# Delta rule stage: inverses of both chunks of a tile in one load, scalings in one load per chunk, each over 128 partitions instead of 64

## The reference

```python
    kk = jnp.einsum('bhnid,bhnjd->bhnij', k, k)
    lower = jnp.where(strict, beta[..., :, None] * kk * decay, 0.0) + jnp.eye(blen, dtype=f32)
    ...
    def step(s, xs):
        u_c, w_c, qk_c, qd_c, kt_c, gt_c = xs
        v_new = u_c - jnp.einsum('bhld,bhde->bhle', w_c, s)
        o_c = jnp.einsum('bhld,bhde->bhle', qd_c, s) + jnp.einsum('bhij,bhje->bhie', qk_c, v_new)
        s = s * gt_c[..., None, None] + jnp.einsum('bhld,bhle->bhde', kt_c, v_new)
        return s, o_c
```

## Time and profile before

| | us |
|---|---|
| three runs | 3799.37, 3775.93, 3805.12 |
| median | 3799.37 |
| the profiled execution, its own time | 3786.45 |
| its span, first to last instruction | 3784.6 |
| mean granted clock of TensorE | 0.953 of full |
| delta stage, from GpSimd's first step in it to its first step in the next | 1770.78 to 2136.54 |

### The profile page before, as it was taken

The page is one execution under the profiler, slowest core; times in us unless marked ns, Lnnn a source line. Parts: engine busy times, 40 slices in busy tenths (PEclk is TensorE's granted clock), DMA queues, the critical chain, the costliest instruction groups (busy, mean ns, idle before and its releaser), DMA issues. The chain is left out here.

```text
span 3784.6 us, 68890 instructions
## 1 busy us (share of the span) xinstructions
PE 3476.5 (92%) x26734; PEld 2979.7 (79%) x26734; DVE 2118.8 (56%) x4012; ACT 1362.6 (36%) x2626; POOL 1028.3 (27%) x1315
## 2 busy tenths in 40 slices
PE   7999999969999999994788569999976999999999
PEld 7999999957877788883777557888865888888887
DVE  6777777638978776932334336666654323233232
ACT  5544554433223232111455406666643111111111
POOL 4222222148988444300577600000000000000000
PEclk9999999989999999996798869999988999999999
DMA  5333333345347444335988222222246111121210
GB/s 158 107 104 111 108 112 107 86 133 179 93 128 213 136 138 121 102 99 118 231 244 248 68 65 96 71 85 72 84 152 224 67 60 67 60 72 59 67 67 35
DMA packets 322211, 429.81 MB, mean 114 GB/s; under 512 B 188587, under 2 KB 206283, under 8 KB 317310
## 3 DMA queue, kind: packets, MB, share of 16 engines
q1 hardware_dynamic: 321926, 425.94, 38.0%
HBM read 268.23 MB, written 160.25 MB: 113 GB/s over the span
## 5 line engine op out<-in xcount | busy, mean ns | idle before, releaser
L88 PE MATMUL b_psP<-b_w_hi,b_xT_hi 128*128 128x512 f32 x1320 | 518.8, 393 | 47.1 <-DVE b_xT_lo L1188 30.1
L89 PE MATMUL b_psP<-b_w_lo,b_xT_hi 128*128 128x512 f32 x1320 | 516.6, 391 | 0.0
L90 PE MATMUL b_psP<-b_w_hi,b_xT_lo 128*128 128x512 f32 x1320 | 516.2, 391 | 0.0
L88 PE MATMUL a_psG<-a_xT_hi,a_w_hi 128*128 128x256 f32 (+1 forms) x1632 | 467.8, 287 | 10.3 <-DVE a_xT_lo L559 9.4
L90 PE MATMUL a_psG<-a_xT_hi,a_w_lo 128*128 128x256 f32 (+1 forms) x1632 | 459.6, 282 | 0.0
L89 PE MATMUL a_psG<-a_xT_lo,a_w_hi 128*128 128x256 f32 (+1 forms) x1632 | 459.5, 282 | 0.0
L88 PEld LDWEIGHTS b_psP<-b_w_hi,b_xT_hi 128*128 128x128 f32 x1320 | 249.6, 189 | 105.7 <-DVE b_xT_lo L1188 53.8
L88 PEld LDWEIGHTS a_psG<-a_xT_hi,a_w_hi 128*128 128x128 f32 x1632 | 309.3, 189 | 26.2 <-DVE a_xT_lo L559 9.8
L576 DVE SCALAR_TENSOR_TENSOR a_act<-a_raw,a_taps,a_act 128x256 f32<-128x256 f32 x576 | 308.6, 536 | 20.5
L90 PEld LDWEIGHTS a_psG<-a_xT_hi,a_w_lo 128*128 128x128 f32 x1632 | 309.6, 190 | 0.0
L89 PEld LDWEIGHTS a_psG<-a_xT_lo,a_w_hi 128*128 128x128 f32 x1632 | 309.5, 190 | 0.0
(11 more groups left out here) (376 smaller groups left out, 7398.5 us busy)
## 6 DMA issues: line engine op xcount, KB each, us to landing
rows_b<-b_rows SPq DMA_DIRECT2D x165, 256.0 KB, 2.2
b_x_full<-xT SPq DMA_DIRECT2D x78, 512.0 KB, 4.0
qkvB<-a_act SPq DMA_DIRECT2D x16, 1536.0 KB, 5.1
d_conv_T<-qkvB SPq DMA_DIRECT2D x16, 1536.0 KB, 11.5
xT<-a_x_full SPq DMA_DIRECT2D x33, 512.0 KB, 5.1
h_mixed<-mixed SPq DMA_DIRECT2D x33, 512.0 KB, 4.0
out<-h_y SPq DMA_DIRECT2D x33, 512.0 KB, 2.9
a_x<-in_x_prompt SPq DMA_DIRECT2D x32, 512.0 KB, 4.6
```

What stands on the lines that cost most here:

```text
L88: nc.tensor.matmul(out, x_hi, w_hi, start=first, stop=False)
L89: nc.tensor.matmul(out, x_hi, w_lo, start=False, stop=False)
L90: return nc.tensor.matmul(out, x_lo, w_hi, start=False, stop=last)
```

## The change

In `load`, the loads of a tile's scalings and matrices are written otherwise. Before, a loop over the two halves of the partitions issued for each half one load of scalings (both chunks, the half's heads, one source row repeated for 64 partitions) and one of matrices (one chunk, 64 partitions). Now a loop over the two chunks issues for each one load of scalings over all 128 partitions, and one load brings the matrices of both chunks to all 128 partitions. The bytes and where each of them ends up are the same. A tile's semaphore now counts three loads instead of four.

```diff
@@ -1418,7 +1418,7 @@
     W = H * C
     HW = W // 2
     BUFS, ZBUFS = 6, 8
-    LOADS = 4
+    LOADS = 3
     with ExitStack() as stack:
         ph = Phase(nc, stack)
 
@@ -1531,11 +1531,12 @@
                     sp.wait_ge(t_o, 2 * 2 * (t - BUFS + 1))
                     sp.wait_ge(g_qd, t - BUFS + 1)
                 ok = c_in[b]
-                for e in range(2):
-                    half = slice(e * C, (e + 1) * C)
-                    sp.dma_start(sc[b][half, :, :, :, :],
-                                 d.kqrow[2 * t:2 * t + 2, e * PAIRS:(e + 1) * PAIRS].partition_broadcast(C)).then_inc(ok, 16)
-                    sp.dma_start(UQ[b][half, :, :, :], d.UQ[:, 2 * t + e]).then_inc(ok, 16)
+                for c in range(2):
+                    sp.dma_start(sc[b][:, c, :, :, :].rearrange("p a x i -> p (a x i)"),
+                                 d.kqrow[2 * t + c].rearrange("(e a) x i -> e (a x i)", e=2).unsqueeze(1)
+                                 .to_broadcast([2, C, PAIRS * 2 * C])).then_inc(ok, 16)
+                sp.dma_start(UQ[b][:, :, :, :].rearrange("p h x i -> p (h x i)"),
+                             d.UQ[:, 2 * t:2 * t + 2].rearrange("j e h x i -> e j (h x i)")).then_inc(ok, 16)
                 if t >= ZBUFS:
                     sp.wait_ge(g_out, t - ZBUFS + 1)
                 sp.dma_start(za[z][:, :], d.rows_b[t * P:(t + 1) * P, 0:W]).then_inc(za_in[z], 16)
```

## The result

The changed kernel takes **4288.3 us** in the median of four runs (4285.44 to 4292.61); the kernel before took 3802.24 beside it. The ratio is **1.129**, with a 95% interval of 1.123 to 1.135: 13% slower. The forecast was 4263 us in a range of 4180 to 4600. The profiled execution is one of the four, 4285.44 us with a span of 4283.6.

A forecast was written before the change was run, and what follows sets the result against it. The changed delta stage was taken to be bound by loads on two DMA engines: 32 tiles at 24.6 us make 787 us, with the tail +473; 3786.45 + 473 + 4 for a slower clock = 4263 us, range 4180 to 4600.

The forecast's parts named there:

- The stage alone is touched: Nothing outside the delta stage moves, apart from 4 us for a slower clock in the next; the stage gets 473 us longer.
- Issues at nothing: SP in the delta stage issues three loads a tile instead of four; put at 0, at most 19 us.
- The cut by the smaller outermost count: New sc and UQ loads count 2 outermost in DRAM, 128 in SBUF; the smaller binds, so two DMA engines carry them.
- 24.6 us a tile: Delta stage: each of two engines carries 606,208 B a tile at 24.6 GB/s; 32 tiles make 787 us.
- the 15.4 of the mix: Lower bound in GB/s for an engine's rate, from the delta stage's busy mix of loads before; it would give 39.4 us a tile.
- The tail: After the last load lands, GpSimd, about five tiles behind, needs 36 us, plus 8 for slow clock and 4 to the next stage.
- What would show it: Signs in the delta stage: DMA 2 tenths near 95 GB/s, line 1611 every 24 to 25 us, long GpSimd waits, clock near 0.5.
- Rival A: Delta-stage loads still use sixteen engines, at 405 GB/s, so compute decides: -47 us, 3739 us; chance 0.10.

The follow-up runs named there:

- e1_matrices_only: Against the kernel before, only the matrices (UQ) come in one load over 128 partitions, scalings as before; 4040.95 us, ratio 1.062.
- e2_scalings_only: Against the kernel before, only the scalings (sc) come in two loads over 128 partitions, matrices as before; 4042.62 us, ratio 1.063.
- q4_other_rows: The changed kernel with 4 instead of 2 outermost on the DRAM side, reading other rows; 3982.23 us, ratio 1.047 to the kernel before.
- rows_together: The changed kernel with matrices and scalings each read from 128 rows lying together in DRAM, other rows; 3756.44 us, ratio 0.987 to the kernel before.
- v1_scalings_copied: The kernel before with scalings copied in DRAM to 16 rows and loaded over 128 partitions, matrices as before; 3802.93 us, ratio 0.999.
- matrices16_other_rows: The kernel before with matrices in one 128-partition load, 16 outermost in DRAM, other rows, scalings as before; 3800.99 us, ratio 0.999.

## Why the prediction was right, step by step

**The stage alone is touched.** Right: 476.9 of the 499.0 us are in it, forecast 473, and 4.1 behind it, forecast 4 for a slower clock. That second agreement is luck as far as is known: in the first 64 us behind the stage TensorE was busy 42.3 us against 42.4 before, at a clock of 0.71 against 0.74, and the rest of the execution behind the stage lasts between 1646 and 1657 us in the fourteen profiles, with no order by the length of the stage. The 18.0 ahead of it are not from the change, and they are most of the 22 us by which the profiled execution lies above the forecast.

**Issues at nothing.** Right in the sum, wrong in its reason. SP does one issue less, but its issues went from a median of 0.6 us to 5.1 for UQ, 5.1 for za and 3.5 for sc. The reason given was that SP waits for buffers; it waited 132.6 us in the stage for TensorE to free them before, and 7.8 us in the changed kernel, where it sits in its issues instead. The prediction did not foresee this. It adds nothing to the sum, because the pace goes by the bytes of the two engines, in `e1_matrices_only` and `e2_scalings_only` too.

**The cut by the smaller outermost count.** Right, and the step on which everything hung. The count was varied and the time followed it from 2 to 16. The Trainium skill (DMA: Bandwidth & Descriptors, "Why a DMA increments its semaphore by 16 and not by 1") has the number of engines as the largest up to 16 that divides the outermost counts of both sides. These runs agree with it for 2, 4, 8 and 16 on the DRAM side against 128 on the other. They can't tell it from the prediction's "the smaller side binds", since each of these counts divides 128.

**24.6 us a tile.** Measured 24.87, so 24.4 GB/s on each of the two engines, 1% under the row taken. To choose the rate of the 128-partition load rather than the 15.4 of the mix was right. Its reason, that with one engine on each half of the partitions nobody is in its way, is not shown: with two engines on each half (`q4_other_rows`) the rate fell only to 22.4, with four to 20.4. The stage's 32 tiles make 796 us instead of 787.

**The tail.** GpSimd was to run five tiles behind the loads, and five tiles follow the last one that waits. From that wait's end at 2588 to the next stage it took 43 us, forecast 48 (36, 8 and 4). The 8 us for the slow clock were more than it took: the tiles after 2588 come 8.0 us apart from the first. From 2590 to 2600 the clock was indeed 0.51, but GpSimd was busy 9.8 of these 10 us, so it set the pace there and not TensorE.

**What would show it.** DMA share 2 tenths and 97 GB/s over some eight slices (forecast 95), a period of 24 to 25 us, hundreds of us of waiting on stores: all there. The clock was forecast near 0.5 in the stage and is 0.59 to 0.64, since TensorE is granted 0.97 in the last part of its work in each period. The 50 us and more in which sc and UQ were to land can't be checked, since the profile gives no landing times for them; za, behind them in the queue, went from 8.4 to 20.9 us.

**Rival A's price.** It was put at -47 us for sixteen engines at the rate of the conv_T load. Sixteen engines over 128 partitions, with blocks 256 KB apart and scalings read eight times, gave 20 us by the timed runs and 33 by the stage; with rows together it was 47 and 50. What the prediction left out is the source: it took the rate of a load whose rows lie together for loads whose rows don't. The Trainium skill (SBUF — State Buffer, "Can I just issue two DMAs to hit both halves?") has it that only one transfer over all 128 partitions reaches all ports. The conv_T load (405 GB/s against 216) agrees with that, and so does the gain of `rows_together`; `v1_scalings_copied` and `matrices16_other_rows` show that for the mix of this stage the gain is not had by halves.

## What to carry to other kernels

Before two loads to halves of the partitions are merged into one, write down what each side of the new transfer counts outermost. If it is 2, two of the sixteen engines do it, however many partitions are written, as here; put a dimension that is a multiple of 16 outermost on both sides, or change the layout in DRAM so that this is possible. And where loads are the limit, look at whether rows lie together and are each read once: here, blocks 256 KB apart and a row read eight times cost a third of the gain by the stage's length (33 us of 50 were left) and over half by the timed runs (0.995 against 0.987).

## What had not been expected of the hardware

- SP's issue of a load took 0.6 us with 16 engines in use, 1.6 with 8, 4.7 with 4 and 5.1 with 2, with the same SBUF side and bytes (UQ, 512 KB). An issue that takes many times its usual time in the trace can be a sign that too few engines stand behind the queue.
- With loads over 128 partitions cut in 16 the stage moved 264 GB/s at a share of 0.86 when rows were far apart and repeated, and 260 at 0.75 when they lay together: 307 against 347 GB/s for a full share.
- One of two kinds of load moved to 128 partitions brought nothing (0.999 twice), both together 0.5%, and 1.3% with rows together.
